# The sampled tokens' cache and state work, spread over three earlier stages of one fused decoder step

## The reference, cut to what matters

```python
z = einsum('bsd,de->bse', rms_norm(h, g_pre), w_in)         # w_in: 2048 x 22528
qa, ka, va, za, qr, kr, vr, zr, ga, gb = split(z)
# attention: 3 groups (window, dilation) = (128,1), (512,4), (2048,16), 8 heads of 128
#   sampled token: 128 cached keys and values of each group and head, and its own row
s = einsum('bshd,bskhd->bshk', q, kg) - slope * offs        # kg: gathered from the cache
o = einsum('bshk,bskhd->bshd', exp(s - m), vg) / den        # mixed over the 3 groups
new_win = concatenate([buf, new_row])[1:]                   # the caches, moved by one row
# retention: 8 heads, state 256 x 256 for each token and head
R = R * gamma_h + k^T v;   yr = q R                          # sampled token: one step
merged = sigmoid(ga) * (ya * silu(za)) @ w_a + sigmoid(gb) * (norm(yr) * silu(zr)) @ w_r
h = h + rms_norm(merged @ w_o);  h = h + sigmoid(h @ w_gate) * (p @ w_proj)
```

## Time and profile before

| what | value |
|---|---|
| time of the runs, median (lowest to highest of 3) | 3314.6 us (3312.48 to 3322.01) |
| span of the profiled execution, first to last instruction | 3308.5 us |
| median run above that span | 6.1 us |
| busy share: PE, DVE, ACT, POOL | 94%, 36%, 26%, 8% |

### The profile page before, as it was taken

How to read it: one execution, slowest core, us unless ns; L and a number is a source line. 1 busy time by engine, 2 the same in 40 slices (tenths; PEclk the granted TensorE clock), 3 DMA queues, 4 the chain that set the end, 5 groups by cost and what they waited for, 6 DMA issues and landing times. The chain is left out here.

```text
span 3308.5 us, 58517 instructions
## 1 busy us (share of the span) xinstructions
PE 3120.6 (94%) x24526; PEld 3036.4 (92%) x24526; DVE 1174.6 (36%) x1387; ACT 857.9 (26%) x1049; POOL 257.2 (8%) x369
## 2 busy tenths in 40 slices
PE   7999999999999999999999998878988899999798
PEld 7999999999999999999999998778988799999698
DVE  5313223132231322232223222555455543422632
ACT  6223222232222222222222222232222221222222
POOL 2000000000000000000000000112111110100310
PEclk9999999999999999999999999888988899999899
DMA  8554545445454454444444454999999665643352
GB/s 298 187 187 145 187 139 187 163 152 179 161 168 161 167 185 163 163 157 160 163 163 157 161 169 91 223 233 237 206 234 223 197 193 162 195 140 127 96 184 89
DMA packets 531395, 574.83 MB, mean 174 GB/s; under 512 B 12584, under 2 KB 492504, under 8 KB 527864
## 3 DMA queue, kind: packets, MB, share of 16 engines
q1 hardware_dynamic: 490944, 428.31, 40.0%
q0 software_dynamic: 40256, 143.45, 17.1%
HBM read 515.45 MB, written 232.42 MB: 226 GB/s over the span
## 5 line engine op out<-in xcount | busy, mean ns | idle before, releaser
L467 PE MATMUL acc<-moving,weights 128*128 128x260 f32 x22080 | 2810.5, 288 | 52.5 <-issue 28.4
L467 PEld LDWEIGHTS acc<-moving,weights 128*128 128x128 f32 x22080 | 2724.4, 191 | 75.8 <-issue 55.4
L1084 DVE TENSOR_TENSOR weights<-raw_weights,weights 128x2048 fp32r<-128x2048 f32 (+1 forms) x242 | 538.7, 2226 | 1401.6 <-ACT weights L801 1383.2
L801 ACT ACTIVATE weights<-raw_weights 128x2048 fp32r<-128x2048 f32 (+1 forms) x242 | 450.9, 1863 | 217.7 <-PE acc L467 208.2
L868 ACT ACTIVATE stage_buffers<-acc 128x520 f32<-128x520 f32 x144 | 87.1, 605 | 1128.1 <-PE acc L467 1127.9
L1566 POOL DMA_DIRECT2D out<-stage_buffers x72 | 52.0, 722 | 1640.2 <-DVEq L1164 873.8
L947 ACT ACTIVATE stage_buffers<-stage_buffers 128x512 f32<-128x512 f32 x64 | 35.1, 619 | 134.8 <-DMA stage_buffers<-vrow_scr 134.8
L1363 DVE SCALAR_TENSOR_TENSOR stage_buffers<-stage_buffers,sampled 128x256 f32<-128x256 f32 x128 | 52.1, 479 | 49.5 <-ACT stage_buffers L947 49.1
L874 ACT ACTIVATE stage_buffers<-stage_buffers,small 128x384 f32<-128x384 f32 (+3 forms) x32 | 32.6, 1019 | 133.1 <-DVE small L1179 133.1
L881 ACT ACTIVATE stage_buffers<-aux 128x384 f32<-128x384 f32 (+2 forms) x72 | 35.4, 491 | 102.9 <-PE aux L559 102.9
L681 PE MATMUL aux<-small,one 8*128 8x8 f32 x48 | 13.3, 359 | 48.4 <-DVEq L1329 48.4
(11 more groups left out here) (195 smaller groups left out, 1587.3 us busy)
## 6 DMA issues: line engine op xcount, KB each, us to landing
raw_weights<-in_w_in SPq DMA_DIRECT2D x176, 1024.0 KB, 5.7
out<-in_cache_win SPq DMA_DIRECT2D x128, 1023.5 KB, 8.4
out<-in_cache_win SPq DMA_DIRECT2D x32, 1022.0 KB, 8.1
stage_buffers<-in_cache_win POOLq DMA_DIRECT2D x48, 512.0 KB, 7.0
stage_buffers<-in_state_ret POOLq DMA_DIRECT2D x16, 1024.0 KB, 7.7
out<-stage_buffers POOLq DMA_DIRECT2D x16, 1024.0 KB, 5.4
raw_weights<-in_w_r_out SPq DMA_DIRECT2D x16, 1024.0 KB, 5.7
raw_weights<-in_w_o SPq DMA_DIRECT2D x16, 1024.0 KB, 5.7
```

The source lines that it names most:

```text
L467: mm = pe.matmul(acc[:, par, half, 0:HC], W[:, par, wp, k, :], U[:, up, k, a:b], start=(k == ks[0] and n == 0), stop=(k == ks[-1] and n == 2))
L801: act.activation(W[:, par, 0, 0:k], raw[:, par, 0:k], ACT.Copy).then_inc(s_whi, 1)
L1084: dve.tensor_tensor(W[:, par, 1, 0:k], raw[:, par, 0:k], W[:, par, 0, 0:k].bitcast(F32), ALU.subtract).then_inc(s_wready, 1)
```

## The change

The order is turned from token by token to head by head, and the work moves to where a head's columns become known:

- **Keys.** In attention head h, TensorE turns the nine sampled tiles of head h-1 (`row_turn`, hook in unit 0), POOL stores the 72 rows, loads for each group 128 keys x 8 tokens (512 KB in rows of 512 bytes) and spreads the query rows (512 KB), and DVE multiplies and reduces before the `lo` of units 2, 4 and 7. Head 7 is done in retention head 0.
- **Softmax.** Once, for all 64 pairs of head and token, in retention head 1, instead of eight times for 8 rows.
- **Values.** Token h-2's values in retention heads 2 to 7, the last two in gate blocks 0 and 1.
- **States.** Head h-1's states in retention head h, in two halves of 4 tokens. A half is now loaded by four transfers of 256 KB and four spread ones of 128 KB, and stored by four of 256 KB. Head 7 is done in gate blocks 0 and 1. Decay is one ACT instruction for a half, with gamma as a per-partition scalar.
- **Hooks.** Each product hook stands in one piece before one tile, with its wait.
- **The rest.** The norm of the sampled rows moves to gate block 1. Gate blocks 2 to 7 and the `w_a` units hold no sampled work. Two cache copies are left in each retention head; the others go one to each unit of the gates, `w_r` and `w_o`. The projected input uses tiles 0 and 1 of `U`, which are filled last. The retention loops of all engines run over 6 heads, with heads 0 and 1 written out.

```diff
 # SP
-                if j < 6:
+                if j < 2:
                     keep_rows(sp, 2, h, 10 + j)
-                else:
-                    keep_rows(sp, 1, h, j - 4)
...
                 load(j % 2, w0, c)
+                keep_rows(sp, 2, i, 12 + j)
...
-                if j == 0:
-                    keep_rows(sp, 1, i, 0)
+                keep_rows(sp, 1, i, j)
 # TensorE
+                **({} if first else {0: {8: [row_turn]}}),
...
+        def sample_states(half):
+            pe.wait_ge(s_rnew, count.due(s_rnew))
+            pe.wait_ge(s_free[3], count.due(s_free[3]))
+            for b in range(HB):
+                for e in range(2):
+                    mm = pe.matmul(aux[:, 3, e * HB + b:e * HB + b + 1], r_v[:, half, b, e * P:(e + 1) * P],
+                                   one[:, 0:1], start=True, stop=True)
+            mm.then_inc(s_full[3], 1)
...
+                0: {8: [row_turn]} if nth == 0 else {12: [sample_scores]} if nth == 1 else {},
+                2: {2: [sample_probs]} if nth == 1 else {8: [sample_values]} if nth == 2 else {},
+                3: {8: [lambda: sample_states(0)]} if nth else {},
                 4: {4: [lambda: ret_rows(rk, 0, 2, 0)], 8: [lambda: ret_rows(rk, 1, 0, 1)],
+                    **({13: [lambda: sample_states(1)]} if nth else {})},
...
-                7: {1: [lambda: ret_values(0)], ...
+                7: {0: [vrow_turn], 1: [lambda: ret_values(0)], ...
...
+        gates({2: {8: [sample_values]}, 3: {8: [lambda: sample_states(0)]}})
+        gates({0: {8: [lambda: sample_states(1)]}, 2: {4: [sample_norm], 12: [sample_values]}})
+        with count.loop(H - 2, ...) as i:
+            gates({})
 # ACT, retention head
+                if nth and j in (2, 3):
+                    scaled_states(j - 2, h - 1)
 # DVE, attention head and retention head
+                if not first and j == 0:
+                    rows_keep()
+                if not first and j in (2, 4, 7):
+                    sample_keys({2: 0, 4: 1, 7: 2}[j], h - 1)
...
+                if nth == 1 and j == 1:
+                    sample_softmax()
+                    sample_normed()
+                if nth == 2 and j == 1:
+                    sample_columns(h - 2)
+                if nth == 2 and j == 3:
+                    sample_output(h - 2)
+                if nth and j in (2, 3):
+                    sample_states(j - 2, h - 1)
+                    sample_queries(j - 2, h - 1)
+                if nth and j in (4, 5):
+                    sample_ret_y(j - 4, h - 1)
 # POOL
+        def states_in(half, h, nth):
+            pool.wait_ge(s_rhalf, count.due(s_rhalf))
+            if nth > 1:
+                pool.wait_ge(s_rnewst[half], count.due(s_rnewst[half], skip=HB - 1))
+            for b in range(HB):
+                pool.dma_start(r_st[:, half, b], state[0, half * HB + b, bass.ds(h, 1)]...).then_inc(s_rst[half], 16)
+            for b in range(HB):
+                pool.dma_start(r_v[:, half, b]..., v_src[b:b + 1].broadcast_to([P, 2, P])).then_inc(s_rst[half], 16)
...
+        def retention_head(h, nth):
+            pool.wait_ge(s_decfree, count.due(s_decfree))
+            pool.dma_start(decay, c_decay[:, bass.ds(h * T, T)]).then_inc(s_decay, 16)
+            ...
+            if nth:
+                states_in(0, h - 1, nth)
+                states_in(1, h - 1, nth)
+                states_out(0, h - 1)
+                states_out(1, h - 1)
+                values_in(h - 1)
+            pool.wait_ge(s_vrow, count.due(s_vrow))
+            store(vrow_scr[...], vrow[0:2 * NS], s_vrowst, s_vrowfree)
```

More of the change, by code:

```diff
@@ L452, in _, with unit @@
         halfcols = [(0, HC), (HC, TC)]
[L454 removed]
+        def unit(par, ks=tuple(range(KD)), hooks=None, tiles_due=None):
             pe.wait_ge(s_wready, count.due(s_wready))
@@ new lines, in sample_scores @@
+        def sample_scores():
+            pe.wait_ge(s_scol, count.due(s_scol))
+            pe.wait_ge(s_free[1], count.due(s_free[1]))
+            for g in range(G):
+                at = g * (NK + 1)
+                pe.transpose(aux[0:NR, 1, at:at + NK], scol[:, g * NR:(g + 1) * NR], ident[:])
+                mm = pe.matmul(aux[0:NR, 1, at + NK:at + NK + 1], qk[:, g * NR:(g + 1) * NR], one[:, 0:1],
+                               start=True, stop=True)
+            mm.then_inc(s_full[1], 1)
@@ L676, in sample_probs @@
[L676 to L700, removed]
-            for e in range(2):
-                mm = pe.matmul(aux[:, 3, 2 * h + e:2 * h + e + 1], r_v[:, half, h, e * P:(e + 1) * P],
-                               one[:, 0:1], start=True, stop=True)
-            if h == HH - 1:
-                mm.then_inc(s_full[3], 1)
-        values = [lambda h=h: sample_values(h) for h in range(0, H, 2)]
@@ L708, in _ @@
-        low, high = ([lambda n=n, half=half: sample_states(half, n) for n in range(HH)] for half in range(2))
-        def gates(first, last):
-            hooks = {
-                0: {9: [sample_rows]} if first else {**{3 + n: [values[n]] for n in range(4)},
-                                                     **{9 + n: [high[n]] for n in range(4)}},
-                2: {8: [sample_scores]},
-                3: {5: [sample_probs], **{7 + n: [low[n]] for n in range(HH)},
-                    15: values if last else []},
-            }
+        retention_head(0)
@@ L742, in _ @@
         unit(1, att_ks)
-        unit(0, att_ks, hooks={4 + n: [high[n]] for n in range(HH)})
-        unit(1, att_ks)
-        unit(0, att_ks, hooks={3: [sample_norm]})
-        unit(1, att_ks)
-        with count.loop(KD // 2 - 3, rates, first=3) as i:
+        with count.loop(KD // 2 - 1, rates, first=1) as i:
             for j in range(2):
@@ L1414, in _ @@
+        gates(0)
+        gates(1)
+        with count.loop(H - 3, [(s_whi, 4)], first=2) as i:
+            gates(2)
+        gates(2, True)
         dve.drain()
@@ new lines, in _ @@
+        gate_store(1, 0)
+        states_out(1, H - 1)
+        for j in range(1, 4):
+            gate_store(1, j)
+        for half in range(2):
+            pool.wait_ge(s_rnewst[half], count.due(s_rnewst[half], skip=HB - 1))
+        pool.wait_ge(s_svfree, NS + 1)
+        for n in range(8, KD):
+            pool.dma_start(y_in[:, n, 0:T], y_scr[H + n]).then_inc(s_yin[1], 16)
+        with count.loop(H - 2, [(s_sg, 4), (s_sgst, 4)], first=2) as i:
+            for j in range(UNITS_GATE):
+                gate_store(i, j)
```

734 lines of the change are left out of this document (378 added, 356 removed).

## The result

The changed kernel takes 3153.8 us at the median (3152.5 to 3156.4) against 3315.9 of the kernel before in the same measurement: a ratio of 0.950, 95% interval 0.949 to 0.952, so 162 us faster.

The account below looks back on a forecast made before the run. The prediction took transfers, met through waits in front of the weight chain, to bound the gate stage, and TensorE elsewhere. Its terms, -175.7 - 16 + 50.5 + 3.5 + 12 = -125.7 us, gave a median of 3189, range 3158 to 3262.

Parts of the forecast that it names:

- Gates and `w_a`: Gate stage and products with w_a, freed of sampled work: gains of 175.7 us (170 to 183) and 16 (12 to 17).
- seven loop turns: Gate stage: the loop over six blocks turns at each end, 1.0 us each, between 0 and 1.89, 7 us in all.
- the new wait: Retention, hook `sample_states(0)` in unit 3: TensorE waits for the states' chain; 1.5 us allowed for each of eight heads, 12.
- The room: Retention: the states' chain ends at 1300.7 and TensorE reaches its hook at 1302.7, so 2 us to spare.
- every bound on its good side: Whole kernel: the time if all bounded terms fall on their favourable side, 3162 us.
- the small turns: Turns of sampled tiles: nine in retention at 0.48 us, 4.5 in all, and seven in attention, 3.5.
- the pieces: Retention: twenty added pieces of `sample_values` and `sample_states` at 2.0 us each cost 40 us (37 to 45).
- softmax: Retention, done once: twelve products cost 5.8 us, plus a wait of 4 (0 to 10) at `sample_probs`.
- front: Program start: tiles 0 and 1 of `U` are filled last but also read last by the first unit; cost 0.
- Late states: Retention: last landing 15 us after its issue, TensorE waits 4.1 us a head and loses clock; 3242 us, chance 0.22.
- both halves land together: Retention: engines share time evenly between halves 0 and 1, TensorE waits 17.6 us a head; 3366 us, chance 0.08.
- Keys do not hold attention: Attention: the rival had DVE's wait for keys show in full before `lo`, 204 us; 3393 us, chance 0.03.

Follow-up runs that it names:

- the plain rows: Kernel before, with the gate stage's two spread loads replaced by loads of the same bytes from a contiguous cache block: ratio 0.962, 127 us faster.

## Where the prediction was right, and why it was 35 us too slow

**Gates and `w_a`: right.** -178.7 against -175.7 (range -170 to -183), -14.8 against -16. Their mechanism, waits for the loads of spread rows and the clock that goes with them, is confirmed by the plain rows, which alone give back 127 us. Blocks without sampled work take 46.1 us. The seven loop turns at 1.0 each do not show there: 46.1 is four units of 11.53.

**The step that failed** is the last one of the new wait: "I allow 1.5 each for the spread of landings: 12". Nothing of it was needed: no head waits in that hook. The chain had been timed from the dear end throughout: a y store at 3.96, measured 2.1 to 2.7; the last landing 9 us after its issue, measured 6.0 in the head shown (1399.35 - 1393.3). Dearer than thought were only the issues, 0.71 for 0.56. The room was 4.3 to 6.1 and not 2, and the landings did not scatter beyond it. An allowance came on top of terms that already held one.

**Why the time fell out of the range.** The allowance alone doesn't explain this: with every bound on its good side the prediction had 3162, and the 12 already at nothing. What went below were terms without bounds or without a place in the sum: the small turns (6 us), the nine turns and the wait of head 0 (3.7), the clock in attention (6.9) and the distance of the median from the span (3.3), with 1.6 more from the pieces, each explained below. Against these 21.5 us, gates, `w_a`, softmax, front and the clock in retention came out 13.3 worse than their good sides. The clock in attention and the distance, 10 us together, are not shown to come from the change; without them the time would be about 3164, inside the range.

**Sizes that were off.** Pieces at 1.77 in place of 2.0: 4.6 over 20. The small turns at 0.48 each, 8 us in all: a unit with `row_turn` took 11.65 where its neighbours took 11.53, so 0.1 each and under 2 in all; a turn that TensorE does not wait for adds only that much here, and the 0.48 of the earlier trace rows had been read behind a wait. Softmax 8.0 in place of 9.8 (the result of the first unit of head 1 steps back by 4.8, though the turn of the loop, 1.9, is gone there, and the third by 1.2); its wait stood in `sample_scores`, 2.7, and not in `sample_probs`. Head 0 lost 3.7 that no term had, the turns and the wait shown above. Gates 3.0.

**Luck.** Attention at the lower clock for 6.8 us in place of 20.5 is 13.7 x 0.5 = 6.9. Over all traces it was 20 to 27 in the four that keep the old attention and 7 to 31 in the eight with the new one: no part of the change is shown to move it. With half of that time taken off, the stage takes 1062 to 1069 in all twelve. The second measurement of the change, at 0.953, would be about 3159, just inside the range.

**Against these** stand 2.0 for the front, where nothing was expected (4.4 at the first result, of which 2.4 are back by the third), some 2.6 left over in retention (heads 5 and 6 spent 6.8 us at the lower clock, which costs 3.4), and 1.2 in `w_a`. Together: 12 + 4.6 + 6 + 1.8 + 3.7 + 3.0 + 6.9 - 5.8 = 32.2 of the 31.8 between the two sums; the other 3 us of the 35 are the distance of the median from the span, 2.8 here and 6.1 before. The 6.1 was no fixed cost: where a time and a span of the same execution are on record they differ by about 1.5, so the profiled execution before was some 4.6 us faster than its median.

**The rivals.** Late states did not happen, though their price, 3 to 8 us of clock, held at its low end (3.2). That both halves land together did not happen: half 0 is complete 11.0 us after the first issue, when half 1 has just been issued. Keys do not hold attention: DVE is busy 49 us more there and POOL 34, the DMA share came to 0.58 and not to 0.70, and attention takes 1069 to 1079 us with them, 1076 to 1079 without.

## What to carry to other kernels

Look at how a transfer reads before counting its bytes: here 24 DRAM rows of 512 bytes spread to all partitions took twice as long as the same bytes in a block, and the waits behind such loads cost the stage a fifth of its time (557.6 to 440.4). When a chain of several steps is timed against a deadline, take each step from the middle of its rows and put the doubt into the range once; bounds taken step by step and then an allowance added counted it twice here. Give every term of a sum its bounds, small ones too: the turns had none, and they helped to carry the time out of the range. And a wait of TensorE can be worth more than its length: 7.0 us of waiting cost 10.3 with the clock here.

## What the runs showed that was not expected

Joining eight transfers into four left the time to complete 1.5 MB where it was (11.0 and 10.4 us). A 4 KB packet of the spread query rows took 728 ns before and takes 162 in the changed kernel, which spreads them too. Lower-clock stretches in attention vary from 7 to 31 us between executions of code that is the same there. And 32 copies of 1 MB cost 76 us in a stage at a DMA share of 0.92, and about 1 in the same units once their other transfers had gone.
